# Expert stage with fixed first blocks, a ring of weight pairs filled from the out-projection on, and token numbers found by one-hot products

## Chip, core and metric

The kernel runs on one core of one Trainium2 chip. The metric is the device time of the whole kernel in microseconds, from the first to the last instruction and what lies around them; lower is better. All arrays are fp32 unless said otherwise.

## What is computed

One step of a one-layer decoder trunk with model width 1024, for 512 prompt tokens and 32 sample tokens (8 sequences of 4) with a paged cache of 2048 past positions each. Cut to what matters here:

```
h = RMSNorm(x)
q, k, v, gates = split(h @ w_in)
o_a = sparse attention over the top keys picked by an indexer   (prompt and sample)
o_b = block-sparse attention over the top blocks                (prompt and sample)
x  += (sigmoid(gate_a) * (o_a @ w_br_a) + sigmoid(gate_b) * (o_b @ w_br_b)) @ w_out
h2  = RMSNorm(x) * g_ffn
per token: best of 4 groups, then the top 2 of its 8 experts, with weights w1, w2
x  += sum over both experts of  w * ((silu(h2 @ w_gate[e]) * (h2 @ w_up[e])) @ w_down[e])
y   = RMSNorm(x) * g_final
```

There are 32 experts of hidden width 256: w_gate and w_up are 1024 x 256 each, w_down 256 x 1024, so 3.1 MB per expert and 100.7 MB for all. 544 tokens with 2 experts each give 1088 assignments.

## The kernel before

The work runs in stages, each a block in which every engine has its own list of instructions. Between two blocks all engines meet; in several places semaphores are reset there as well. Nothing is reordered by a planner: the order on each engine and each queue (SP's, ACT's and POOL's) is the order written, and waits are on semaphores written by hand. `Chain` (L130) makes each VectorE instruction wait for the one before it.

`project` (L269) normalises x and multiplies by w_in for the attention columns. At its start POOL also writes 25 blocks of rows with the number NOROW into `slot_table` in HBM (L387 to L391), beside the first loads of x, constants and weights. `prompt` does the prompt's attention.

`sample` (L906) does the sample's attention. TensorE goes through NS steps: `turn(n)` transposes gathered keys, `scores(n-1)` multiplies them by queries; ScalarE copies each turned tile out. VectorE picks the top keys by repeated rounds of eight (`rounds`), merges the lists (`largest_of_all`), counts, and lets TensorE add up the counts in `places_left`, which stands in front of step COUNT_AT (L925). VectorE's list is `rounds(0, 24)`, `mask(0)`, `normalise(0)` (which waits for ScalarE's `exps(0)`, L1255), the other eight rounds, `largest_of_all`, `bias_of_choice`, `mask(1)` and so on (L1398 to L1410). The bias is used by `spread` (L1101). The value gathers are issued by POOL as slots of the ring of eight come free. At the end `weigh(3, 1)` is the last product with gathered values, and then TensorE turns the outputs o_b and o_a into obT and oaT (L1191 to L1201).

`merge` (L1419) makes u column block by column block (8 blocks of 128 columns). Per block j TensorE makes the two gate products (i = 0, 1) and the two branch products (i = 2, 3), each in two halves of 272 tokens. For the gate products hT and the gate weights are split by VectorE into a high and a low part in fp32r, and each product is three (L1545); the branch products are plain fp32 (L1536). SP loads gate weights into one buffer and branch weights into two. ScalarE makes the sigmoids, VectorE multiplies and adds. Then, in the same block, comes the out-projection, token tile by token tile (5 tiles): uT times w_out, added to x (which has been loaded over hT), RMSNorm, store of h2 and of x to HBM by SP (L1511, L1513), transposes of h2 and the router product.

`route` (L1694) is a chain of small VectorE instructions: group and expert choice as one-hot arrays E[0], E[1]; a product with a triangular matrix counts the earlier assignments (L1750); from it the place of each assignment in a table of blocks of 64 rows, one or more blocks per expert. POOL scatters the token numbers into `slot_table` by ten indirect DMAs (L1853). `block_expert` names the expert of each block, `npair` the number of block pairs.

`experts` (L1858) reads the slot table back (L1903) and loops over the pairs at run time (Fori). SP loads, per turn, the gate and up weights of the two blocks' experts in two parts of 4 k-tiles and the down weights; there is one buffer of each, so a part is loaded again once the products that read it are done. POOL gathers the pair's 128 rows of h2 and scatters the result rows. TensorE turns the rows (L1965), makes gate and up (L1975: 32 products in which the two blocks use the two halves of the array's columns), turns the hidden rows (L1981) and makes down (L1991). Gather, products and scatter of a turn follow one another, except that the next gather is issued once the rows are turned.

`combine` (L2027) loads the expert rows, adds them with w12 to x (loaded again from HBM by SP at the end of `experts`, L1921), normalises and stores.

## Time and profile before

| | us |
|---|---|
| median of 3 runs (range) | 1274.71 (1272.75 to 1276.52) |
| the profiled execution | 1271.91 |
| its span, first to last instruction | 1270.1 |
| TensorE busy, of the span | 1000.6 (79%) |
| VectorE / ScalarE / GpSimd busy | 423.9 / 291.5 / 183.7 |
| granted TensorE clock, mean | 0.883 |
| moved by DMA | 253.05 MB, mean 199 GB/s |

The stages on this clock: project and prompt until 336, sample until 622, merge from 624 to 795, out-projection until 880, routing and the first loads until 935, expert loop until 1240, combine until the end.

How to read the rows. A timeline row has the start, the length (of a merged run, from its first start to its last end), the engine, the line of the kernel, the operation, what it writes and reads, the shape, the count, and in brackets how long the engine had been idle before it and what ended that. PE is TensorE's products, PEld its weight loads, DVE VectorE, ACT ScalarE, POOL GpSimd, SPq the DMA issues of SyncE. A row of a stretch has start and end, the length, the busy time of PE, PEld, DVE, ACT and POOL with their counts, the granted TensorE clock (1.00 is 2.4 GHz, 0.50 is 1.2 GHz), the mean busy share of the 16 DMA engines, and the GB/s that they moved.

### The profile page before, as it was taken

How to read it: one execution, taken by the hardware profiler on the slowest of the kernel's cores; microseconds unless marked ns; L12 is line 12 of the kernel's file. 1: busy time of each engine (PE TensorE's matmuls, PEld its weight loads, DVE VectorE, ACT ScalarE, POOL GpSimd, SP SyncE). 2: the span in 40 equal slices, each digit the busy share in tenths (PEclk: the TensorE clock that was granted, in tenths of full speed). 3: DMA queues.
4: the chain of work that ended last, by engine and by line, in shares of the span. 5: the costliest groups of instructions: out<-in, count | busy, mean ns of one | idle time of the engine just before them, and what ended most of it. 6: DMA issues, size and time to landing. Idle time of an engine off the chain costs nothing. (4 is left out here: it accounts for less than half of the span.)

```text
span 1270.1 us, 14844 instructions
## 1 busy us (share of the span) xinstructions
PE 1000.6 (79%) x5669; PEld 582.1 (46%) x5669; DVE 423.9 (33%) x909; ACT 291.5 (23%) x451; POOL 183.7 (14%) x246
## 2 busy tenths in 40 slices
PE   5999998888899978876499999996057777777750
PEld 4544443667656645123399999453022222222220
DVE  2214886444349282220333330122401111111116
ACT  3122212444247747010100000111001110110112
POOL 4100100120013324333100000000301111111110
PEclk9999999998599979687799999997569988898895
DMA  8212201223149948998583330110199999999985
GB/s 292 84 67 75 94 1 38 59 65 109 67 144 336 374 150 303 399 387 308 151 286 86 98 89 1 45 72 26 19 316 373 372 349 369 350 366 366 366 311 211
DMA packets 147382, 253.05 MB, mean 199 GB/s; under 512 B 20096, under 2 KB 111632, under 8 KB 139008
## 3 DMA queue, kind: packets, MB, share of 16 engines
q1 hardware_dynamic: 124800, 149.05, 35.2%
q0 software_dynamic: 21904, 101.02, 21.9%
q10 hardware_dynamic: 624, 2.23, 0.5%
q8 instruction: 38, 0.62, 0.2%
q14 instruction: 16, 0.13, 0.0%
HBM read 240.46 MB, written 20.19 MB: 205 GB/s over the span
## 5 line engine op out<-in xcount | busy, mean ns | idle before, releaser
L679 PE MATMUL bank<-ring,hT 128*128 128x512 f32 (+1 forms) x384 | 162.5, 578 | 1.6 <-DMA ring<-in_w_in 1.6
L1975 PE MATMUL bank<-w_gate_up,xT 128*64 128x512 f32 x512 | 127.7, 651 | 32.6 <-DVE xT L2016 20.9
L679 PEld LDWEIGHTS bank<-ring,hT 128*128 128x128 f32 x384 | 72.7, 194 | 81.9 <-issue 71.4
L1245 ACT COPY kT_s<-bank 128x1024 f32<-128x1024 f32 (+1 forms) x90 | 85.7, 997 | 64.0 <-PE bank L1030 63.9
L1030 PEld LDWEIGHTS bank<-consts,ring 128*128 128x128 f32 x704 | 79.8, 146 | 41.3 <-ACT kT_s L1245 35.1
L1030 PE MATMUL bank<-consts,ring 128*128 128x128 f32 x704 | 91.7, 284 | 2.7 <-PEq L219 1.7
L1975 PEld LDWEIGHTS bank<-w_gate_up,xT 128*64 128x64 f32 x512 | 38.1, 149 | 112.2 <-issue 91.4
L1545 PE MATMUL bank<-hT_hi,gate_w_hi 128*128 128x272 f32 x256 | 76.1, 297 | 14.8 <-DVE gate_w_lo L1645 14.8
L1991 PE MATMUL bank<-w_down,hidT 128*64 128x512 f32 x256 | 70.1, 697 | 9.8 <-DVE hidT L2023 8.5
L1545 PE MATMUL bank<-hT_hi,gate_w_lo 128*128 128x272 f32 x256 | 74.6, 291 | 0.0
L1545 PE MATMUL bank<-hT_lo,gate_w_hi 128*128 128x272 f32 x256 | 74.6, 291 | 0.0
L1583 PE MATMUL bank<-w_o,uT 128*128 128x512 f32 (+1 forms) x160 | 69.5, 593 | 1.7 <-DVE uT L1664 1.7
L1149 PE MATMUL bank<-ring,wT_s 128*32 128x512 f32 x256 | 48.4, 926 | 21.3 <-DMA ring<-in_cache_v_b,rows_b 21.3
L2016 DVE COPY xT<-bank 128x1024 f32<-128x1024 f32 x16 | 19.6, 1224 | 123.9 <-PE bank L1965 123.9
L1965 PE MATMUL bank<-consts,xg 128*128 128x128 f32 x128 | 19.8, 305 | 49.8 <-DMA xg<-h_rows,id 49.7
L1545 PEld LDWEIGHTS bank<-hT_hi,gate_w_hi 128*128 128x128 f32 x256 | 49.1, 192 | 15.2 <-DVE gate_w_lo L1645 14.9
L2019 DVE TENSOR_TENSOR sgm<-sgm,bank 128x256 f32<-128x256 f32 x16 | 6.7, 421 | 147.5 <-ACT sgm L2004 147.5
L1853 POOL DMA_INDIRECT slot_table<-rt_ids,slot x10 | 10.9, 1089 | 296.3 <-DVE rt_ids L1834 293.6
L1545 PEld LDWEIGHTS bank<-hT_lo,gate_w_hi 128*128 128x128 f32 x256 | 49.1, 192 | 0.3
L1545 PEld LDWEIGHTS bank<-hT_hi,gate_w_lo 128*128 128x128 f32 x256 | 49.0, 191 | 0.0
L265 POOL DMA_INDIRECT ring<-in_cache_k_b,rows_b x32 | 30.0, 937 | 128.4 <-PE bank L1030 98.7
L1583 PEld LDWEIGHTS bank<-w_o,uT 128*128 128x128 f32 (+1 forms) x160 | 27.5, 174 | 40.9 <-issue 40.9
(329 smaller groups left out, 1378.0 us busy)
## 6 DMA issues: line engine op xcount, KB each, us to landing
w_gate_up<-in_w_e_gate SPq DMA_DIRECT2D x64, 512.0 KB, 7.9
w_gate_up<-in_w_e_up SPq DMA_DIRECT2D x64, 512.0 KB, 8.9
w_down<-in_w_e_down SPq DMA_DIRECT2D x32, 1024.0 KB, 10.4
ring<-in_w_in SPq DMA_DIRECT2D x5, 2048.0 KB, 8.3
gate_w<-in_w_in SPq DMA_DIRECT2D x16, 512.0 KB, 5.2
w_o<-in_w_out SPq DMA_DIRECT2D x1, 4096.0 KB, 14.9
ring<-in_x_prompt SPq DMA_DIRECT2D x4, 512.0 KB, 8.4
branch_w<-in_w_br_a SPq DMA_DIRECT2D x16, 128.0 KB, 3.4
```

The lines of the kernel that those rows point to most:

```text
L265: pool.indirect_dma_start(s.ring[:, r, 0:wide], None, cache.rearrange("g (p e) h d -> (g p) (e h d)", e=e), bass.IndirectOffsetOnAxis(inde ...
L679: last = nc.tensor.matmul(bank[:, n % 4, 0:WID[g]], s.hT[:, k, t * P:(t + 1) * P], w[:, gi % 2, k, 0:WID[g]], start=(k == 0), stop=(k == K ...
L1030: last = nc.tensor.transpose(bank[:, u, e * P:(e + 1) * P], ring[:, slot, at:at + P], ident)
L1149: last = nc.tensor.matmul(out[rows_at(u), :], probT[m][:, c * nslot + e, rows_at(u)], ring[:, slot, e * w:(e + 1) * w], start=(c == 0 and ...
L1245: nc.scalar.copy(kT[:, n % 2, u, :], bank[:, u, :]).then_inc(kT_kept, 1)
L1545: last = nc.tensor.matmul(out, l, m, start=(k == 0 and c == 0), stop=(k == KD - 1 and c == 2))
L1583: last = nc.tensor.matmul(bank[0:rows, n % 4, :], uT[:, k, t * P:t * P + rows], wo[:, k, half * 512:half * 512 + 512], start=(k == 0), sto ...
L1853: pool.indirect_dma_start(s.slots, bass.IndirectOffsetOnAxis(ap=s.slot[0:rows, k, t:t + 1], axis=0), ids[0:rows, k, t, :], None).then_inc( ...
L1965: last = nc.tensor.transpose(bank[:, k // 4, k % 4 * PAIR:(k % 4 + 1) * PAIR], xg[:, k * P:(k + 1) * P], const(s, "ident"))
L1975: last = nc.tensor.matmul(bank[r, 2, :], xT[:, kk, r], wgu[:, u, part, k, :], start=(kk == 0), stop=(kk == KD - 1))
L1991: last = nc.tensor.matmul(bank[r, 4 + half, :], hidT[:, f, r], wd[:, u, f, half * 512:half * 512 + 512], start=(f == 0), stop=(f == KF - 1))
L2016: nc.vector.tensor_copy(xT[:, :, :].rearrange("p (b k) r -> p b (k r)", b=2), bank[:, 0:2, :])\
```

## The change

In words, with the new names:

- `project`: the 25 zero-row stores, `slot_table` and `residual_rows` are gone. The constants lose 80 columns and gain 193.
- `sample`: SP gets a block that loads the branch weights of column block 0 into `s.bw`. COUNT_AT is NI + 38 instead of NI + 33; `exps(0)` comes one step earlier; VectorE's order changes; `weigh(3, 1)` moves behind the turning of o_b.
- `merge` ends before the out-projection. Column block 0 does the branches first and its gate products plain, from an unsplit buffer `gw0` that lies in w_out's place; gate loads run one block further ahead; w_out is loaded at block 3, x at block 5.
- `project_out`, a new block, is the out-projection as it was, except that x is not stored, POOL stores h2, and SP issues gate/up weights of pairs 0 and 1 and down weights of pair 0.
- `experts` now holds the routing too. Blocks 0 to 31 are the first 64 rows of expert 0 to 31, whatever their count; further rows go to overflow blocks (at most 16). The first 15 pairs are unrolled, with weights in a ring of three gate/up pairs (two in `s.early`, one in w_out's place) and two down pairs (one in uT's place). The sixteenth pair and the overflow pairs are a run-time loop with at least one turn. The routing places give a row and a block number for each assignment; ten pairs of products of one-hot matrices put token number + 1 (+ 2048 for the second choice) into PSUM, and six VectorE instructions make gather and scatter numbers of it. Rows and results have two buffers each; the next pair's rows are turned between gate/up and the hidden rows.
- `combine` reads x from where it stayed in SBUF.

Sampling:

```diff
@@ sample @@
-    COUNT_AT = NI + 33
+    COUNT_AT = NI + 38
...
+        @block.sync
+        def _(sp):
+            for half in range(2):
+                sp.dma_start(s.bw[half * HD:half * HD + HD, 0, 0, :, :],
+                             a["w_br_a"][0, half * PAIRS * HD:(half + 1) * PAIRS * HD, 0:P]
+                             .rearrange("(j d) n -> d j n", d=HD)).then_inc(first_in, 16)
+            sp.dma_start(s.bw[:, 0, 1, :, :], a["w_br_b"][0, :, 0:P].rearrange("(j p) n -> p j n", p=P))\
+                .then_inc(first_in, 16)
+            sp.wait_ge(first_in, 48)
...
-            weigh(3, 1)
             pe.wait_ge(spread_read, 10)
             for x in "ba":
+                if x == "a":
+                    weigh(3, 1)
...
-                if n == NI + 26:
+                if n == NI + 25:
                     exps(0)
...
             mask(0)
+            rounds(FIRST_ROUNDS, TOPK_S // 8 - FIRST_ROUNDS)
             normalise(0)
-            rounds(FIRST_ROUNDS, TOPK_S // 8 - FIRST_ROUNDS)
             largest_of_all()
+            mask(1)
             bias_of_choice()
-            mask(1)
             normalise(1)
```

Merge and out-projection:

```diff
@@ merge @@
+        gw0 = wo[:, 0:2, :].rearrange("p g (k n) -> p g k n", k=KD)
+        ORDER = [(2, 3, 0, 1)] + [(0, 1, 2, 3)] * (NCH - 1)
...
             gates(0)
-            branches(0)
+            gates(1)
             branches(1)
-            gates(1)
-            sp.dma_start(wo[:, :, :], a["w_out"][0].rearrange("(k p) n -> p k n", p=P)).then_inc(out_in, 16)
-            sp.wait_ge(hT_split, KD)
-            sp.dma_start(xp, a["x_prompt"][0].rearrange("(t p) d -> p t d", p=P)).then_inc(x_in, 16)
-            sp.dma_start(xs[:, :], a["x_sample"].rearrange("b q d -> (b q) d")).then_inc(x_in, 16)
             for c in range(2, NCH):
                 gates(c)
                 sp.wait_ge(prod_done, 4 * (c - 1))
                 branches(c)
+                if c == 3:
+                    sp.wait_ge(hT_split, KD)
+                    sp.dma_start(wo[:, :, :], a["w_out"][0].rearrange("(k p) n -> p k n", p=P)).then_inc(s.out_in, 16)
+                if c == 5:
+                    sp.dma_start(s.xp, a["x_prompt"][0].rearrange("(t p) d -> p t d", p=P)).then_inc(s.res_in, 16)
+                    sp.dma_start(s.xs[:, :], a["x_sample"].rearrange("b q d -> (b q) d")).then_inc(s.res_in, 16)
...
+                            if j == 0:
+                                last = nc.tensor.matmul(out, gw0[:, i, k, :], s.hT[:, k, rows],
+                                                        start=(k == 0), stop=(k == KD - 1))
+                                continue
@@ project_out, SP and POOL @@
+            sp.dma_start(gf[:, :], a["g_ffn"].to_broadcast([P, D])).then_inc(gf_in, 16)
+            sp.dma_start(wr[:, :, 0:NG], a["w_grp"][0].rearrange("(k p) n -> p k n", p=P)).then_inc(r_in, 16)
+            sp.dma_start(wr[:, :, NG:NG + NE], a["w_exp"][0].rearrange("(k p) n -> p k n", p=P)).then_inc(r_in, 16)
+            load_gate_up(sp, s, a, 0)
+            load_gate_up(sp, s, a, 1)
+            load_down(sp, s, a, 0)
...
+            for t in range(TT):
+                rows = rows_of(t)
+                pool.wait_ge(h2_ready, t + 1)
+                pool.dma_start(s.h2[t * P:t * P + rows, :], h2[0:rows, t % 2, :]).then_inc(h2_stored[t % 2], 16)
```

Experts, loads and token numbers (`load_gate_up` issues four loads of 1 MB, `load_down` two):

```diff
@@ experts, SP @@
+            load_gate_up(sp, s, a, 2)
+            load_down(sp, s, a, 1)
+            for p in range(NGU, LAST):
+                sp.wait_ge(gu_done, p - NGU + 1)
+                load_gate_up(sp, s, a, p)
+                sp.wait_ge(y_done, p - 1 - NWD + 1)
+                load_down(sp, s, a, p - 1)
+            sp.wait_ge(y_done, LAST - 1 - NWD + 1)
+            load_down(sp, s, a, LAST - 1)
+            sp.wait_ge(turns_ready, 1)
+            turns = sp.value_load(nturn[0:1, 0:1], min_val=1, max_val=1 + MAXOB // 2)
+            with sp.Fori(0, turns) as i:
...
+                load_gate_up(sp, s, a, LAST, e)
+                sp.wait_ge(y_done, LAST - NWD + 1)
+                sp.wait_ge(down_free, i + 1)
+                load_down(sp, s, a, LAST, e)
@@ experts, PE @@
+            for k in range(2):
+                pe.wait_ge(places_ready, k + 1)
+                for t in range(TT):
+                    for u in range(2):
+                        column = blocks_are[k][:, t, :].rearrange("p (b u) -> p u b", u=2)[:, u, :]
+                        last = nc.tensor.matmul(bank[half(u), 7, 0:MAXP], rows_are[k][:, t, :], column,
+                                                start=(k == 0 and t == 0), stop=(k == 1 and t == TT - 1))
+            last.then_inc(found, 1)
...
+            turn_tokens(0, 16)
+            for p in range(LAST):
+                gate_up(p, p, 64 * (p // NGU + 1), gu_done)
+                turn_tokens(p + 1, 16 * ((p + 1) // 2 + 1))
+                turn_hidden(p)
+                down(p, p, 32 * (p // NWD + 1), p - 1 if p >= 2 else None, y_done)
@@ experts, DVE, behind the choice of experts @@
+            for k in range(2):
+                link(nc.vector.tensor_tensor(rows_are[k], rowf[:, k, :].unsqueeze(2).to_broadcast([P, TT, BLK]),
+                                             const(s, "iota").unsqueeze(1).to_broadcast([P, TT, BLK]), ALU.is_equal))
+                link(nc.vector.tensor_tensor(blocks_are[k], blkf[:, k, :].unsqueeze(2).to_broadcast([P, TT, NBLK]),
+                                             const(s, "iota")[:, 0:NBLK].unsqueeze(1).to_broadcast([P, TT, NBLK]),
+                                             ALU.is_equal))
+                link(nc.vector.tensor_tensor(blocks_are[k], blocks_are[k],
+                                             const(s, f"word{k}").unsqueeze(2).to_broadcast([P, TT, NBLK]), ALU.mult),
+                     places_ready)
```

VectorE's chain between the sum of the counts and these lines: base (6 instructions), the places (9 of 160 elements a partition, and small sums), the overflow blocks of each expert (2 of 256, a scan and small ones), block number by comparison with 47 block starts (2 of 470) and the row in the block.

## Rows read from the trace of the kernel before

**Rows 1.** Stretches: length, busy PE PEld DVE ACT POOL, granted clock, DMA share, GB/s.

```profile
795.00:880.00 85.00, 82.44 (x280) 40.89 (x280) 15.04 (x26) 13.01 (x31) 0.00 (x0) 0.98 0.14 53
...
880.00:935.00 55.00, 3.53 (x14) 2.76 (x16) 21.13 (x71) 2.99 (x4) 13.61 (x16) 0.50 0.30 88
...
935.00:1240.00 305.00, 221.56 (x920) 78.13 (x920) 38.61 (x63) 41.57 (x47) 38.53 (x63) 0.90 1.03 355
```

**Rows 2.** Short stretches of the expert loop, same columns.

```profile
936.00:938.00 2.00, 2.00 (x6) 0.48 (x4) 0.00 (x0) 0.00 (x0) 0.00 (x0) 0.50 1.04 409
...
948.00:950.00 2.00, 2.00 (x8) 0.87 (x6) 0.00 (x0) 0.00 (x0) 0.00 (x0) 0.50 1.10 349
...
953.85:1027.37 73.52, 53.12 (x232) 19.17 (x232) 9.96 (x16) 12.07 (x14) 10.78 (x17) 0.95 1.07 370
```

**Rows 3.** Timeline, POOL and PE, first 25 us.

```profile
1.49 13.44 POOL L391 DMA_DIRECT2D slot_table<-zrow  x25 [0.32 <-POOL zrow L387]
...
17.21 7.40 PE L679 MATMUL bank<-ring,hT 128*128 128x328 f32 x16 [1.56 <-DMA ring<-in_w_in]
```

**Rows 4.** Timeline, DVE, sampling.

```profile
445.70 0.17 DVE L1384 RECIPROCAL inv_s<-total_s 128x1 f32<-128x1 f32 x1 [12.25 <-ACT lg_b L1208]
```

**Rows 5.** Timeline, PE, sampling, in order of time.

```profile
372.95 1.05 PE L1053 MATMUL bank<-kT_s,q_b 128*32 128x512 f32 x4
...
469.94 0.59 PE L1097 MATMUL bank<-counts,consts 128*128 128x1 f32 x2 [9.25 <-DVE counts L1335]
...
470.82 1.95 PE L1030 MATMUL bank<-consts,ring 128*128 128x128 f32 x8
...
477.12 1.97 PE L1030 MATMUL bank<-consts,ring 128*128 128x128 f32 x16
```

**Rows 6.** Timeline, PE, end of sampling.

```profile
613.34 3.54 PE L1149 MATMUL bank<-ring,kT_s 128*32 128x128 f32 x64 [3.93 <-DMA ring<-in_cache_v_a,rows]
```

**Rows 7.** Timeline, PE, ACT and PEld, merge.

```profile
636.37 0.59 PE L1545 MATMUL bank<-hT_hi,gate_w_hi 128*128 128x272 f32 x1 [14.79 <-DVE gate_w_lo L1645]
...
650.59 0.62 ACT L1602 ACTIVATE sig<-bank 128x544 f32<-128x544 f32 x1 [5.41 <-PE bank L1545]
...
669.99 0.62 ACT L1602 ACTIVATE sig<-bank 128x544 f32<-128x544 f32 x1 [5.41 <-PE bank L1545]
...
766.63 3.52 PEld L1536 LDWEIGHTS bank<-oaT,branch_w 128*128 128x128 f32 x16
```

**Rows 8.** Timeline, first instructions behind two block boundaries.

```profile
624.40 0.21 DVE L1641 MEMSET logit<- 128x180 f32 x1 [2.10 <-PEq L207]
...
880.19 1.28 ACT L1742 ACT_TABLE_LOAD   x1 [0.84 <-PEq L224]
```

**Rows 9.** Timeline, DVE and PE, routing and first turn.

```profile
892.14 0.09 DVE L1804 MEMSET rt_base<- 128x32 f32 x1 [0.81 <-PE bank L1751]
...
900.74 0.82 DVE L1831 TENSOR_SCALAR rt_ids<-consts 128x640 int32<-128x640 f32 x1
...
901.60 0.17 DVE L1834 CAST rt_ids<-consts 128x5 int32<-128x5 f32 x1
...
931.51 1.94 PE L1965 MATMUL bank<-consts,xg 128*128 128x128 f32 x8 [39.52 <-DMA xg<-h_rows,id]
...
934.84 10.09 PE L1975 MATMUL bank<-w_gate_up,xT 128*64 128x512 f32 x32 [1.40 <-DVE xT L2016]
```

**Rows 10.** DMA issues (count, median us from issue to landing).

```profile
xg<-h_rows,id POOLq DMA_INDIRECT x17, 7.1
ring<-in_cache_k_idx,rows POOLq DMA_INDIRECT x16, 3.3
```

**Rows 11.** Timeline, PE, a down product group in the loop.

```profile
1040.46 3.65 PE L1991 MATMUL bank<-w_down,hidT 128*64 128x512 f32 x16 [0.61 <-DVE hidT L2023]
```

**Rows 12.** Waits of PE, 880 to 1240 us (total, times, longest).

```profile
PE bank L1981 <- DVE hid L2021: 23.7, 16, 1.5
```

**Rows 13.** Timeline, ACT, last copy of y.

```profile
1231.69 1.01 ACT L2007 COPY y<-bank 128x1024 f32<-128x1024 f32 x1 [5.84 <-PE bank L1991]
```

More of the change, by code:

```diff
@@ L1520, in _ @@
             for j in range(NCH):
[L1521 removed]
+                for i in ORDER[j]:
                     if i < 2:
[L1523 to L1525 removed]
+                        if j == 0:
+                            pe.wait_ge(gate0_in, 32)
+                        else:
+                            pe.wait_ge(gate_split, 2 * (j - 1) + i + 1)
+                    elif i == 2 and j >= 1:
+                        pe.wait_ge(br_in[j % 2], 48 * ((j + 1) // 2))
                     if j >= 1:
@@ L1547, in _ @@
                     last.then_inc(prod_done, 1)
-            pe.wait_ge(out_in, 16)
-            pe.wait_ge(u_ready, NCH)
+        @block.scalar
+        def _(act):
+            for j in range(NCH):
+                if j >= 2:
+                    act.wait_ge(u_ready, j - 1)
+                for i in range(2):
+                    act.wait_ge(prod_done, 4 * j + ORDER[j].index(i) + 1)
+                    nc.scalar.activation(sg[:, j % 2, i, :].rearrange("p (b r) -> p b r", b=2),
+                                         bank[:, 2 * i:2 * i + 2, 0:HALF], ACT.Sigmoid).then_inc(sig_ready, 1)
@@ new lines, in _, with split, split_gates @@
+        @block.vector
+        def _(dve):
+            link = Chain(dve, chain_v)
+            link(nc.vector.memset(s.logit[:, :, :], 0.0))
+            def split(hi, lo, v, ready):
+                link(nc.vector.tensor_copy(hi.bitcast(F32R), v))
+                link(nc.vector.tensor_tensor(lo.bitcast(F32R), v, hi, ALU.subtract), ready)
+            def split_gates(j):
+                dve.wait_ge(gate_in, 32 * j)
+                for g in range(2):
+                    split(gh[:, j % 2, g, :, :], gl[:, j % 2, g, :, :], gw[:, g, :, :], gate_split)
+            for k in range(KD):
+                split(hTh[:, k, :], hTl[:, k, :], s.hT[:, k, :], hT_split)
+            for j in range(NCH):
+                if j + 1 < NCH:
+                    split_gates(j + 1)
+                for i in (0, 1):
+                    dve.wait_ge(prod_done, 4 * j + ORDER[j].index(i + 2) + 1)
+                    dve.wait_ge(sig_ready, 2 * j + i + 1)
+                    dst = (uT[:, j, :] if i == 0 else part[:, :]).rearrange("p (b r) -> p b r", b=2)
+                    link(nc.vector.tensor_tensor(dst, sg[:, j % 2, i, :].rearrange("p (b r) -> p b r", b=2),
+                                                 bank[:, 4 + 2 * i:6 + 2 * i, 0:HALF], ALU.mult), mul_done)
+                link(nc.vector.tensor_tensor(uT[:, j, :], uT[:, j, :], part[:, :], ALU.add), u_ready)
@@ L1744, in _, with sigmoid, keep @@
             nc.scalar.activation(ratio[:, :], ratio[:, :], ACT.Exp).then_inc(gexp_ready, 1)
-        @block.tensor
-        def _(pe):
-            pe.wait_ge(both_ready, 1)
-            flat = both[:, :, :].rearrange("p t e -> p (t e)")
-            nc.tensor.matmul(bank[:, 0, 0:TT * NE], const(s, "before"), flat, start=True, stop=True)
-            nc.tensor.matmul(bank[:, 1, 0:TT * NE], s.ones[:, :], flat, start=True, stop=True).then_inc(sum_done, 1)
+            def sigmoid():
+                nc.scalar.activation(sgm[:, :], bank[:, 2, 0:DE], ACT.Sigmoid).then_inc(sig_ready, 1)
+            def keep(slot, done, count):
+                act.wait_ge(done, count)
+                nc.scalar.copy(y[:, slot % 2, :].rearrange("p (b n) -> p b n", b=2),
+                               bank[:, 4 + 2 * (slot % 2):6 + 2 * (slot % 2), :]).then_inc(y_ready, 1)
+            for p in range(LAST):
+                act.wait_ge(gu_done, p + 1)
+                sigmoid()
+                if p >= 2:
+                    act.wait_ge(y_stored[p % 2], 16 * (p // 2))
+                keep(p, y_done, p + 1)
+            act.wait_ge(turns_ready, 1)
+            turns = act.value_load(nturn[0:1, 0:1], min_val=1, max_val=1 + MAXOB // 2)
+            with act.Fori(0, turns) as i:
+                act.wait_ge(gu_free, i + 2)
+                sigmoid()
+                act.wait_ge(y_stored[LAST % 2], i * 16 + 16 * (LAST // 2))
+                keep(LAST, down_free, i + 2)
         @block.vector
@@ L2027, in combine @@
+            with dve.Fori(0, turns) as i:
+                hidden(i + LAST)
+                keep_tokens(i + (LAST + 1), LAST)
 def combine(nc, s, a, o):
```

622 lines of the change are left out of this document (299 added, 323 removed).

## Prediction

> **What bounds the kernel now.** I read the page first (the span in 40 slices), then stretches, then the timeline of each stretch. From 935 to 1240 us, in the 16 turns of the expert loop, the DMA share is 1.03 and TensorE is busy 222 of 305 us [rows 1]: the weights' stream sets the pace. When it does not pause it moves 370 GB/s; alone, gate and up weights (1 KB pieces) run at about 350 and down weights (4 KB pieces) at about 410 [rows 2]. Ahead of it, 880 to 935, no engine works much and DMA has a share of 0.30; and 795 to 880, the out-projection, TensorE is busy 82 of 85 us at a DMA share of 0.14 [rows 1]. So the stream is idle for 140 us and then binds for 300. That is the place to look; the other parts of the change touch waits of TensorE.
>
> The reference, run on its inputs, gives 1088 assignments over 32 experts, the largest expert has 50, none is empty. So 32 blocks, 16 pairs, both before and after, and the new loop makes one turn. All 100.7 MB of weights still come once.
>
> **The change, part by part** (times on the clock of the profiled execution).
>
> *Start.* 25 stores of zero rows leave POOL's queue (1.6 MB in 13.4 us) while TensorE's first projection product waits for w_in until 17.2 [rows 3]. At the stream's 370 GB/s [rows 2] they are worth 4.4 us of loads; bounds 0 (something else comes last) and 5. I take 3.0, nearer the upper end because the product's wait ends with a DMA. The constants grow by 113 columns (58 KB, 0.2 us of stream, under the same loads).
>
> *Sampling, the count.* VectorE's normalise(0) waited 12.25 us for ScalarE [rows 4]; the rounds behind it, and so the counts, were late, and TensorE stood 9.25 us at places_left [rows 5]. After it the clock was at the lower level: from 470.82 to 477.12 it did 12 transposes and two steps' scores in 6.3 us, which at 0.12 us a transpose and 1.0 us a step's scores, as elsewhere [rows 5], is 3.4; and places_left itself costs 0.9 instead of 0.4. The new order runs all rounds first (counts ready near 458) and asks five steps later, near 473; exps(0) comes one step earlier on ScalarE, between the same copies. Gain 9.25+2.85+0.4 = 12.5. mask(1) now stands before bias_of_choice: it needs the last b scores (about 467) and takes 10 us, so the bias comes near 482, before its first use near 491: nothing late. The gathers of values start as soon as slots are freed, so they shift too. Bounds 0 (a later wait takes it) and 13.
>
> *Sampling, the tail.* weigh(3,1) waited 3.9 us for gathered values [rows 6]; the 16 b products (0.12 each, 2.0 us) now lie in it. But the a products then wait for VectorE's last read: gain 1.2 (0 to 2.0).
>
> *Merge.* TensorE waited 14.8 us for splits of hT and gates, then took 14 us for the gates and 7.3 for branches; ScalarE's second sigmoid of column block 0 is at 650.6, block 1's at 670.0, so block 1 begins at 657.6 [rows 7]. Now branch weights are there, branches go first (from 624.5, 32 products; 16 weight loads take 3.52 us at the higher clock [rows 7], so 0.227 a product, double for the first 4.2 us): until 633.9. The first gates are unsplit: 32 products at 0.227, 7.3 us, not 96 split ones, which take the rest of a block, 19.4-7.3 = 12.1, until 641.2. Gate loads (1 MB, first in SP's queue: 3 us of stream and a start) are there by about 630; splits for block 1 end at 638.3, both before need. Gain 16.4 (12 to 17). w_out and x move later in SP's queue, behind the branches of blocks 3 and 5; there are 19 us a block and w_out's 4.2 MB need 11 at 370: hidden. Without that cover it would cost its 11. Block 0's branch weights (0.5 MB) come during sampling from SP's queue, which was empty there.
>
> *A new block boundary* between merge and out-projection. Boundaries idle 0.84 and 2.10 us [rows 8]. Route and expert blocks fuse, but their boundary is counted below. Cost 1.8 (0.8 to 4, with the clock falling).
>
> *Out-projection.* SP issues 10.5 MB (two gate/up pairs, one down) in a stretch with DMA share 0.14: 28 us of stream inside 85, nothing waits. Stores of h2 go to POOL's queue, whose engine is empty; the residual's stores are gone. 6.3 MB more go out at 880 (17 us) and are in at about 902. Cost 0; if the covers fail, 45 us (16.8 MB at 370).
>
> *Routing.* Before, VectorE's chain from 892.14 ended at 901.8, then ten scatters, a boundary, a table read, a gather: first transposes at 931.51, first gate/up product at 934.84 [rows 9]. Now: by size (5 elements a partition cost 0.2, 640 cost 0.86 with the gap [rows 9], 160 by the line between them 0.36) the new chain is 12 ops of up to 32 (2.3), 9 of 160 (3.2), two of 256 (0.9), two of 470 (1.4), and per k 320, 240, 240 elements (2.8): 10.6 us, from 891.9 to 902.6. Ten products (1.5), six small ops (1.3): 905.4. Gather without a stream beside it: 3.3 us, as the index gathers; beside the stream it was 7.1 [rows 10], the upper bound. Then 3.3 us to the first product, as before: 912.1. Gain 22.7 (18 to 26). w12 and the block table move behind: covered by the gather and later turns. Without that cover, 4 us.
>
> *Experts.* The stream restarts when gate_up(0) ends, 10.5 us later (10.1 [rows 9], at the lower clock). Left are 13 gate/up pairs and 14 down pairs, 83.9 MB, and 8.1 MB of gathers and scatters: 92.0 MB at 370 = 249 us. Is it fed? Load p waits for product p-3, and a full-clock pair takes TensorE 3.65 for the 16 down products, 7.1 for gate and up (32 products of the same size, 7.3 by twice that) and 1.2 for transposes [rows 5, 11], plus 1.6 of waits (1.5 for hid before, part now under the transposes [rows 12]), 13.6 us, below 18.5 per pair: each load is issued before the stream reaches it. VectorE's copy of xT stands behind hidT's, under the down product. SP's wait for y_done has only the next down load behind it, with one gate/up pair in flight. ScalarE's copy of y waits for the store two pairs back. After the last byte: gate_up(15), hidden, down, copy: 12 us with a dip of the clock. Sum 10.5+249+12 = 271.5 against 934.84 to 1232.70 = 297.9 [rows 9, 13]. Gain 26.4 (16 to 45).
>
> First the row: a stream that does not pause is 370 GB/s. By the Trainium skill, DMA: Bandwidth & Descriptors, Specifications, a core's share of HBM is about 358 GB/s; the stream would then be 257 us, 8 more. The rows disagree [rows 2], the 410 most.
>
> *Combine.* Residual stays on chip: five loads less, which had been under the last turn. Gain 0; one more reset: cost 1.0.
>
> **Sum**: -3.0-12.5-1.2-16.4+1.8-22.7-26.4+1.0 = -79.4. The profiled execution took 1271.9 us (span 1270.1), 2.8 below the median of the runs: 1192.5 on its own scale, 1195 on the median's. I give 1193.
>
> **Rivals.**
> 1. *The stream keeps its old mean*, 355 GB/s over the whole stage [rows 1], pauses included: 92.0/0.355 = 259, +10: 1203. For it: 1 KB pieces again. Against: pauses came from single buffers. Chance 0.12. The Trainium skill's 358 GB/s (DMA: Bandwidth & Descriptors, Specifications) comes to nearly this.
> 2. *The sampling wait only moves*: bias_of_choice is now 7 us later, values become the wait. +12.5: 1205. Against: the slack worked out above. 0.10.
> 3. *The stream is faster*, 400 GB/s with larger loads: 230 us, -19: 1174. 0.08.
> 4. *The clock decides (slower)*. TensorE waits for weights about 5 us per pair. At the lower clock the pair costs 2 x 11.95 + 1.6 = 25.5 us. If the clock were low throughout, the last copy would be at 912+16 x 25.5+2 = 1322 instead of 1184: 1330. Slower than now needs 80 us more, 5.0 per pair over 16.9: 21.9, that is 70% of the work at the lower level. For it: the first product took 10.1 us instead of 7.1 [rows 9, 11]. Against: in the same regime of waits the mean clock is 0.90 [rows 1]. Half of the work low gives 19.5 a pair, 42 more in all: 1235. Chances 0.05 for this half case (0.01 of it near no change), 0.04 for slower. The Trainium skill, TensorE: Matmul & The Clock Gate, HAM oscillation, tells of a kernel that started every tile cold after a DMA wait; the trace agrees only in part, by that 0.90.
> 5. *It does not do what it says*: the early loads are not early (queue or bias loads held up): +45: 1238. 0.04.
>
> **Numbers.** The forecast has 0.57 with its own range 1178 to 1207; the likeliest is the predicted time. Low end 1172 holds rival 3; high end 1220 holds 1 and 2 and part of the half case. About 0.3% (4 us) is what a measurement tells from no change. Faster: all but rival 4's slower case and the 0.01: 0.95; same 0.01; slower 0.04.
>
> **What would show it.** no 9 us wait at the counts; the first merge product near 624.5-16.7 = 608, and from it to the second column block 17 us, where 33 lay between the block's start and that point; first gate/up product 32 us after the out-projection's end, not 55; DMA share above 1 from ten us after it for about 250 us; time from first gate/up to the last y copy 271. If the last is near 298 the experts' term is wrong; if the granted clock in the stage is below 0.8, rival 4 is at work; a wait of TensorE for down weights in each pair is expected, one for gate/up weights is not.

## The result and the profile after

The changed kernel took 1191.5 us (median of four, 1189.3 to 1194.8), the kernel before 1275.6: ratio 0.9346, 95% interval 0.9318 to 0.9374. On two other chips the changed kernel had 1195.8 against 1273.7 (0.9393, 0.9342 to 0.9445) and 1199.7 against 1273.9 (0.9420, 0.9374 to 0.9466). Forecast were 1193 and a range of 1172 to 1220. One of e11's six runs below, at 1189.3 us, was slow as a whole, with a granted clock of 0.887 where the others had 0.900 to 0.916, and is left out of e11's median.

The profiled execution took 1191.2 us, with a span of 1189.3; before, 1270.1. Cut at the first or last product of each stage, the difference of 80.8 us lies here (all times are TensorE's, in us; each row runs from the point that the row above names to its own):

| from ... to | before | after | difference | forecast |
|---|---|---|---|---|
| start, first projection product | 17.2 | 13.0 | -4.2 | -3.0 |
| first query product of sampling | 327.2 | 322.9 | -4.3 | 0 |
| end of the last score product | 158.3 | 147.2 | -11.1 | -12.5 |
| end of sampling's last product | 118.8 | 112.5 | -6.4 | -1.2 |
| first out-projection product | 173.8 | 165.3 | -8.5 | -14.6 |
| first gate/up product | 139.5 | 118.9 | -20.6 | -22.7 |
| end of the last down product | 296.7 | 271.1 | -25.6 | -26.4 |
| end | 38.5 | 38.5 | 0.0 | +1.0 |

The sum is right to 1.4 us, and that is partly luck: the merge gave 6 us less than forecast, and the two stages for which little or nothing was forecast (to the first query product, and the second part of sampling) gave 9.5 us more.

Stretches of the changed kernel, with the columns of [rows 1]: the out-projection, the routing, the stretch from about the landing of the last early weights to the end of the first gate/up products, and the expert stage.

```profile
760.83:845.43 84.60, 82.30 (x280) 40.71 (x280) 14.83 (x25) 13.01 (x31) 2.71 (x5) 0.98 0.47 159
845.43:879.69 34.26, 5.93 (x52) 4.89 (x52) 21.27 (x77) 2.99 (x4) 2.82 (x4) 0.50 0.62 202
862.00:888.00 26.00, 12.81 (x80) 6.41 (x80) 11.50 (x36) 0.00 (x0) 3.09 (x3) 0.60 0.27 91
888.00:1140.00 252.00, 195.88 (x852) 71.32 (x852) 35.98 (x60) 20.94 (x30) 28.58 (x30) 0.89 1.05 364
```

The out-projection takes as long as before, 83.6 us from its first product to the end of its last router product (83.8 before), with 159 GB/s beside it instead of 53: the early loads cost nothing there. From 888 on the stream does not pause (share 1.05) and moves 364 GB/s for 252 us. But from 867, when the last early weights land, to 888.3, when SP issues the next ones, it stands, because every buffer is full and none is free before the first gate/up products have ended.

TensorE's timeline at the counts, and then at the merge's first column block:

```profile
465.25 0.38 PE L1114 MATMUL bank<-counts,consts 128*128 128x1 f32 x2
465.49 0.36 PE L1115 MATMUL bank<-counts,consts 128*128 128x1 f32 x2
...
597.88 6.31 PE L1523 MATMUL bank<-oaT,branch_w 128*128 128x272 f32 x16 [2.33 <-PEq L217]
604.03 3.83 PE L1523 MATMUL bank<-obT,branch_w 128*128 128x272 f32 x16
607.69 14.83 PE L1528 MATMUL bank<-hT,w_o 128*128 128x272 f32 x64
622.16 0.49 PE L1534 MATMUL bank<-hT_hi,gate_w_hi 128*128 128x272 f32 x1
```

The wait of 9.25 us of [rows 5] is gone, and the products of the counts take 0.4 us and not 0.6: the clock did not fall. In the merge, look at the count of L1528 (a count is of records, the instructions as the profile lists them). The 32 plain gate products of the code (2 gates, 2 halves, 8 k-tiles) are 64 records and take 14.8 us, not the 7.3 that the prediction gave them. Column block 1 begins 24.3 us after the first product, not 17.

The routing, first on VectorE and then on TensorE:

```profile
849.42 0.35 DVE L2025 TENSOR_TENSOR logit<-logit,router_bias 128x180 f32<-128x180 f32 x1 [9.43 <-DMA router_bias<-in_b_exp]
...
857.86 0.09 DVE L2052 MEMSET rt_base<- 128x32 f32 x1 [1.44 <-PE bank L1917]
...
868.03 0.41 DVE L2087 TENSOR_TENSOR branch_w<-branch_w,consts 128x240 f32<-128x240 f32 x1
...
870.96 0.18 DVE L2098 SCALAR_TENSOR_TENSOR ids<-id_second,id_found 128x24 int32<-128x24 f32 x1
```

```profile
876.34 1.97 PE L1930 MATMUL bank<-consts,oaT 128*128 128x128 f32 x8 [6.58 <-DMA oaT<-h_rows,ids]
879.69 8.53 PE L1939 MATMUL bank<-early,obT 128*64 128x512 f32 x32 [1.39 <-DVE obT L2124]
```

From the start of the base at 857.86 to the last one-hot matrix is 10.6 us and to the token numbers 13.3, to 0.2 us as worked out from sizes. The gather then takes 5.2 us until its rows can be turned, not 3.3. The first line shows a wait that both kernels have: the chain starts 4.0 us behind the start of the block (3.3 before), because the router's bias is loaded there.

In the expert stage, a pair with its wait (TensorE), the last copy of y (ScalarE, the answer to [rows 13]), and the list of TensorE's waits from 860 to 1160 us:

```profile
949.54 6.01 PE L1958 MATMUL bank<-early,hidT 128*64 128x512 f32 x16 [7.34 <-DMA early<-in_w_e_down]
955.38 7.03 PE L1939 MATMUL bank<-w_o,obT 128*64 128x512 f32 x32
```

```profile
1150.92 1.01 ACT L1989 COPY branch_w<-bank 128x1024 f32<-128x1024 f32 x1 [5.79 <-PE bank L1958]
```

```profile
PE bank L1958 <- DMA early<-in_w_e_down: 23.8, 5, 7.3
PE bank L1958 <- DMA uT<-in_w_e_down: 23.3, 6, 5.0
...
PE bank L1939 <- DMA early<-in_w_e_up: 1.0, 1, 1.0
```

As forecast, TensorE waits for down weights and, but for 1.0 us at the last pair, not for gate and up. The forecast had this wait in each pair; it is in 11 of 16. In nine pairs the down products behind it run at the lower level in part (5.2 to 6.7 us instead of 3.65; 6.0 above), and it costs nothing: the gate/up products start at once behind them, and the next pair's down weights are waited for again, 2.8 to 5.0 us, in all nine.

### The profile page after: what moved, and what is told of

It reads as the page before. It is cut to its first block and busy times, and to the rows that moved or that the text cites. A ratio compares the mean times of both kernels' runs of the same rounds, so it can differ in the third digit from the quotient of the medians.

```text
span 1189.3 us, 14006 instructions
## 1 busy us (share of the span) xinstructions
PE 981.8 (83%) x5685; PEld 577.0 (49%) x5685; DVE 420.8 (35%) x912; ACT 272.6 (23%) x436; POOL 155.2 (13%) x183
## 3 DMA queue, kind: packets, MB, share of 16 engines
q0 software_dynamic: 21408, 101.05, 23.1%
## 5 line engine op out<-in xcount | busy, mean ns | idle before, releaser
L686 PEld LDWEIGHTS bank<-ring,hT 128*128 128x128 f32 x384 | 72.0, 192 | 79.4 <-issue 70.4
L1939 PE MATMUL bank<-early,obT 128*64 128x512 f32 x352 | 79.0, 602 | 2.4 <-DVE obT L2124 1.4
L1534 PE MATMUL bank<-hT_hi,gate_w_hi 128*128 128x272 f32 x224 | 65.9, 294 | 0.0
L1534 PE MATMUL bank<-hT_hi,gate_w_lo 128*128 128x272 f32 x224 | 64.6, 288 | 0.0
L1534 PE MATMUL bank<-hT_lo,gate_w_hi 128*128 128x272 f32 x224 | 64.5, 288 | 0.0
L1958 PE MATMUL bank<-early,hidT 128*64 128x512 f32 x128 | 39.4, 772 | 25.6 <-DMA early<-in_w_e_down 23.8
L1958 PE MATMUL bank<-uT,hidT 128*64 128x512 f32 x128 | 39.4, 773 | 24.5 <-DMA uT<-in_w_e_down 23.3
L1939 PEld LDWEIGHTS bank<-early,obT 128*64 128x64 f32 x352 | 26.1, 140 | 53.7 <-issue 50.0
L1989 ACT COPY branch_w<-bank 128x1024 f32<-128x1024 f32 x16 | 16.2, 1012 | 153.0 <-PE bank L1958 153.0
L1880 POOL DMA_INDIRECT expert_rows<-branch_w,ids x15 | 15.1, 1006 | 227.2 <-ACT branch_w L1989 227.2
L853 ACT ACTIVATE prob<-bank,ntop 128x512 f32<-128x512 f32 (+3 forms) x64 | 30.2, 523 | 53.5 <-DVE ntop L893 53.5
## 6 DMA issues: line engine op xcount, KB each, us to landing
early<-in_w_e_down SPq DMA_DIRECT2D x16, 1024.0 KB, 12.7
```

Of the source, the lines that this page charges most:

```text
L686: last = nc.tensor.matmul(bank[:, n % 4, 0:WID[g]], s.hT[:, k, t * P:(t + 1) * P], w[:, gi % 2, k, 0:WID[g]], start=(k == 0), stop=(k == K ...
L853: nc.scalar.activation(prob[:, m % 3, half, 0:width(t)], bank[:, 2 * (m % 2) + half, 0:width(t)], ACT.Exp, bias=ntop[:, m % 4, half:half + ...
L1534: last = nc.tensor.matmul(out, l, m, start=(k == 0 and c == 0), stop=(k == KD - 1 and c == 2))
L1880: pool.indirect_dma_start(s.y, bass.IndirectOffsetOnAxis(ap=column, axis=0), y[:, p % 2, :], None, bounds_check=2 * NTOK - 1, oob_is_err=F ...
L1939: last = nc.tensor.matmul(bank[half(u), 2, :], xT[:, slot % 2, k, half(u)], gate_up_at(s, slot)[:, u, k, :], start=(k == 0), stop=(k == KD ...
L1958: last = nc.tensor.matmul(bank[half(u), 4 + 2 * (slot % 2) + n, :], hidT[:, f, half(u)], down_at(s, slot)[:, u, f, n * 512:n * 512 + 512], ...
```

## Experiments

Each edit is made to the changed kernel.

**e1 and e10, the zero rows.** A scratch array takes them:

```diff
+            nc.gpsimd.memset(zrow[:, :], NOROW).then_inc(zero_ready, 1)
+            pool.wait_ge(zero_ready, 1)
+            for k in range(25):
+                pool.dma_start(s.slots[k * P:(k + 1) * P, :], zrow[:, :]).then_inc(zero_done, 16)
```

> The changed kernel with the 25 stores of zero rows (1.6 MB) back on POOL's queue at the start; nothing else differs. In the changed kernel the first projection product begins at 13.0 us, before at 17.2, and sampling's first transposes come 7.8 us earlier. Theory 1 (the stores took the loads' place in the DMA engines, and TensorE starts later and at the lower clock): first projection product at 17, whole kernel +5 to +8 us. Theory 2 (my prediction's size): +3 us. Theory 3 (the earlier start is something else, the stores are free): within 1 us.

Measured: 1203.6 us, ratio 0.9475 (0.9441 to 0.9509), 12.3 above e3 below, which ran on the same chip and whose time is the changed kernel's. But the profiled execution had 1194.5 at a granted clock of 0.910, and the four others 1203.4 to 1206.5 at 0.895 to 0.900. So it was taken again with the changed kernel (e9) beside it.

> The changed kernel itself again, beside the next three: 1188 to 1198 us, first gate/up product to last down product 271 to 273 us, out-projection to first gate/up product 118.4 to 118.9 us, as in its two traces.

> The zero-row stores back at the start, as in e1, where the trace showed 5.3 us at the second token tile of the projection (24.06 against 18.74) and the medians of two different chips 8 to 12. Theory 1 (the trace has it all, the rest was the chip and the clock in the prompt's stage): +5 to +6 us against the changed kernel on the same chip. Theory 2 (the later start also costs clock in the stages that follow): +8 us or more.

Measured: e10 1205.5 us (0.9465, 0.9421 to 0.9509), e9 1199.7 (0.9420, 0.9374 to 0.9466; 1.7 above what was expected, with its two stages, 272.2 and 118.5 us, as expected): 5.8 apart, as theory 1 has it, and the intervals overlap. TensorE's timelines, e9 first, then e10:

```profile
14.36 5.09 PE L686 MATMUL bank<-ring,hT 128*128 128x328 f32 x16
19.29 1.04 PE L652 MATMUL bank<-consts,ring 128*128 128x128 f32 x8
```

```profile
15.63 6.31 PE L694 MATMUL bank<-ring,hT 128*128 128x328 f32 x16 [1.24 <-DMA ring<-in_w_in]
21.78 1.04 PE L660 MATMUL bank<-consts,ring 128*128 128x128 f32 x8
```

With the stores the wait for w_in is back and the first 16 products run partly at the lower clock; the second tile begins 2.5 us later (in e1, against the changed kernel's first trace, 5.3). The first product begins at 15.6 and, in e1, at 17.5 us, in the eleven traces of the changed kernel and its versions without the stores at 13.0 to 14.6, with no wait for w_in. So it is shown that the stores hold up the first loads: theory 3 is out. The size is not settled. The timelines have 2.5 to 5.3 us, the medians 5.8 and 12.3, and the difference goes with the granted clock of later stages, which theory 2 claims and which varies by itself as well (last section).

**e2, sampling's order.**

```diff
-    COUNT_AT = NI + 38
+    COUNT_AT = NI + 33
-                if n == NI + 25:
+                if n == NI + 26:
             mask(0)
-            rounds(FIRST_ROUNDS, TOPK_S // 8 - FIRST_ROUNDS)
             normalise(0)
+            rounds(FIRST_ROUNDS, TOPK_S // 8 - FIRST_ROUNDS)
             largest_of_all()
-            mask(1)
             bias_of_choice()
+            mask(1)
```

> The changed kernel with sampling's old order: the counts asked five steps earlier, exps(0) one step later, normalise(0) between the rounds, bias_of_choice ahead of mask(1). Theory 1 (the wait at the counts comes back and nothing behind it hides it): a wait of 8 to 10 us of TensorE at the product of the counts and +11 to +13 us in all, of which 12.5 was my term. Theory 2 (a later wait for gathered values takes most of it, as the values' stage got only 3 us shorter): +3 to +8 us.

```profile
473.71 0.59 PE L1114 MATMUL bank<-counts,consts 128*128 128x1 f32 x2 [9.26 <-DVE counts L1353]
```

Measured: 1208.5 us (0.9500, 0.9466 to 0.9534), against 1191.3 for e3 on the same chip. The wait came back, 9.26 us where it had been 9.25: theory 1, though more than its 11 to 13 us in all. From the first query product to the end of the last score product the stage takes 158.2 us, as before the change (158.3); the changed code takes 147.2 to 150.2 in its twelve other traces (every other run here leaves that stage as it is). From there to the end of sampling it is 115.3, inside the 109 to 119 of the others. So the order is worth 8 to 11 us and nothing behind it takes them back. The values' stage differs from trace to trace by as much as the 5 us that it seemed to gain. The medians are 17 apart; the rest is not explained by the edit's own stage, and stages before it differ as much by themselves (last section).

**e3, the first gates.** Split in three as in the other blocks:

```diff
-                        if j == 0:
-                            pe.wait_ge(gate0_in, 32)
-                        else:
-                            pe.wait_ge(gate_split, 2 * (j - 1) + i + 1)
+                        pe.wait_ge(gate_split, 2 * j + i + 1)
...
-                            if j == 0:
-                                last = nc.tensor.matmul(out, gw0[:, i, k, :], s.hT[:, k, rows],
-                                                        start=(k == 0), stop=(k == KD - 1))
-                                continue
```

> The changed kernel, branches of column block 0 still first, but its gate products split in three as in every other block, with its gate weights loaded into the common buffer. A plain product is two records of 0.227 us in the trace, 32 of them 14.5 us; a split one is three of 0.126, 32 of them 12.1 us, but they can start only when VectorE has split hT and the weights, about 12 us after the block begins, 2 us behind the branches. Theory 1 (the plain form gains nothing, all of the gain comes from the branches' place): column block 1 begins within 1 us of the changed kernel's 24.3 us after the first branch product, time within 1 us. Theory 2 (my prediction's: plain gates save the splits' wait and 4.8 us): +5 us or more.

```profile
603.61 3.83 PE L1518 MATMUL bank<-obT,branch_w 128*128 128x272 f32 x16
609.53 0.39 PE L1527 MATMUL bank<-hT_hi,gate_w_hi 128*128 128x272 f32 x1 [2.08 <-DVE gate_w_lo L1548]
```

Measured: 1191.3 us (0.9367, 0.9334 to 0.9400). The wait for the splits is 2.1 us, and the split products win it back: ScalarE's second sigmoid of the block comes 24.60 us after the first branch product, in the changed kernel 24.68. Plain gates gain nothing; all of the merge's 9 us are the branches that stand where the wait was. Theory 1.

**e4, late loads.**

```diff
@@ project_out, SP @@
-            load_gate_up(sp, s, a, 0)
-            load_gate_up(sp, s, a, 1)
-            load_down(sp, s, a, 0)
@@ experts, SP, behind the loads of the biases @@
+            load_gate_up(sp, s, a, 0)
+            load_gate_up(sp, s, a, 1)
+            load_down(sp, s, a, 0)
```

> The changed kernel with the 10.5 MB of early weights (two gate/up pairs, one down pair) loaded at the start of the routing and not in the out-projection. Theory 1 (the stream is a fixed amount of work behind routing: every MB loaded early is time saved): +28 us. Theory 2 (the stream stands idle from 862 to 888 us in the changed kernel, because all buffers are full until the first gate/up products are done; the 10.5 MB would mostly fall into that gap): 16.8 MB from 846 on at 365 GB/s end at 892, 4 us after the time at which the stream restarts now: +3 to +8 us. Theory 3 (the first gate/up product or the gather of rows is delayed by the stream beside it): up to 4 us more than theory 2.

The gather now runs beside the stream:

```profile
875.65 1.97 PE L1930 MATMUL bank<-consts,oaT 128*128 128x128 f32 x8 [9.86 <-DMA oaT<-h_rows,ids]
```

And the stretch from 862 to 888, in which the changed kernel moved 91 GB/s, is full:

```profile
862.00:888.00 26.00, 13.50 (x85) 6.97 (x86) 7.86 (x28) 0.39 (x1) 3.09 (x3) 0.62 1.08 364
```

Measured: 1197.9 us (0.9432, 0.9394 to 0.9470), 6.6 above e3 on the same chip. In the trace, out-projection to first gate/up is 122.1 us (+3.2: TensorE waits 9.86 us and not 6.58 for the rows, and the first two gathers take 7.5 and 7.7 us to land where they took 4.2 and 4.4), and the expert stage is 276.7 (+5.6). Theories 2 and 3, not 1: moving 10.5 MB out of an idle stretch costs 7 to 9 us and not 28, since the stream has another idle stretch, 867 to 888, that takes most of them. The out-projection without the early loads beside it takes 83.8 us, with them 83.6.

**e5 and e6, the ring.** e5 is the changed kernel again.

> The changed kernel itself, on the chip of the next three kernels, to compare them with: 1188 to 1195 us. In the profiles so far the stage from the prompt's attention to sampling's first score product is up to 11 us longer or shorter with the same instructions, at another granted clock; a span of this run within that.

Measured: 1195.8 us, 0.8 above what was expected, and 272.8 us for the expert stage. e6 has

```diff
-NGU, NWD = 3, 2
+NGU, NWD = 2, 2
...
-            load_gate_up(sp, s, a, 2)
             load_down(sp, s, a, 1)
```

> The changed kernel with two gate/up buffers and not three (both still loaded in the out-projection; w_out's place stays empty; one more wait ahead of the last pair's loads). Theory 1 (stream bound; a ring of two keeps it fed, as a pair's products take 13 us of the stream's 17; only the 4.2 MB loaded during routing come later): 4.2 MB at 365 GB/s = +11 to +12 us, DMA share above 1.0 as before. Theory 2 (the third buffer is what keeps the stream from pausing): pauses of 2 us or more in each of 14 pairs on top, +35 us or more, DMA share below 1.0.

```profile
890.00:960.00 70.00, 54.45 (x248) 20.75 (x246) 9.59 (x16) 5.59 (x8) 8.11 (x8) 0.90 0.99 335
960.00:1150.00 190.00, 140.71 (x578) 48.51 (x576) 23.98 (x40) 13.97 (x20) 19.25 (x19) 0.86 1.05 364
```

Measured: 1209.5 us (0.9507, 0.9443 to 0.9571), +13.7; the stage 285.5, +12.7. The second row has the same 364 GB/s as with three buffers; only its start is thinner. Theory 1, with a little more than its 11 to 12 us: the third buffer is worth the 4.2 MB that it holds early (11.5 us at 365 GB/s), not a steadier stream.

**e7 and e11, the pieces.** Each partition takes neighbouring rows of the weights instead of every 128th, and the tokens are turned with the same stride, so the sums are over the same terms in another order:

```diff
-    return w.rearrange("p (u k n) -> p u k n", u=2, k=KD)
+    return w.rearrange("p (u c k n) -> p u c k n", u=2, c=2, k=KD)
...
-            w = a[name][0].rearrange("e (k p) n -> p e k n", p=P)
+            w = a[name][0].rearrange("e (p k) n -> p e k n", p=P)
...
-                                               xg[:, slot % 2, k * P:(k + 1) * P], const(s, "ident"))
+                                               xg[:, slot % 2, :].rearrange("p (q k) -> p k q", k=KD)[:, k, :],
+                                               const(s, "ident"))
```

and likewise for down (not in e11).

> The changed kernel with the experts' weights laid out so that a partition's share of a load is one piece of 8 KB in HBM and in SBUF (partition p holds rows 8p to 8p+7 of gate or up, 2p and 2p+1 of down, instead of every 128th row; the tokens and hidden rows are turned with the same stride). Before, gate/up pieces are of 1 KB and down pieces of 4 KB, and moved at about 350 and 410 GB/s. Theory 1 (the stream binds and its rate goes by the size of the pieces): gate/up rise to about 400: 54.5 MB behind the restart in 136 instead of 152 us, the stage 15 to 20 us shorter, DMA rate 390 to 410. Theory 2 (the mix is limited elsewhere, at 365 to 370 whatever the pieces): within 3 us. Theory 3 (strided reads of the rows slow the transposes): they take longer than 1.1 us for eight, hidden under the stream's waits.

> As e7, but only gate and up get pieces of 8 KB; down keeps its pieces of 4 KB. Theory 1 (the 1 KB pieces of gate and up were the slow ones, 4 KB is long enough): same as e7 within 2 us: first gate/up product to last down product 245 to 247 us, rate about 410 GB/s. Theory 2 (the rate still rises from 4 to 8 KB): e7 keeps 4 us or more of its 27.

The stage's stretch of e7, of e11, and of e12 below:

```profile
888.00:1110.00 222.00, 185.46 (x833) 72.86 (x833) 35.82 (x60) 19.54 (x28) 27.28 (x27) 0.93 1.00 413
```

```profile
888.00:1110.00 222.00, 185.10 (x814) 69.53 (x812) 33.57 (x56) 18.92 (x28) 26.34 (x26) 0.92 0.98 398
```

```profile
890.00:1110.00 220.00, 182.19 (x816) 72.03 (x818) 34.44 (x58) 19.58 (x28) 27.34 (x27) 0.92 1.01 416
```

Measured: e7 1172.5 us (0.9227, 0.9170 to 0.9283), 23.4 under e5 on the same chip, stage 245.2 (-27.6), more than the 15 to 20 us of its theory 1. e11 1175.8 us (0.9242, 0.9187 to 0.9298), 24.0 under e9, stage 249.0 (-23.1). The stream is what binds, and its rate goes with piece length: 364 GB/s with gate and up in pieces of 1 KB, 398 with 8 KB, 413 with down in 8 KB as well. The last step is worth 2 to 4 us in the stage (249.0 against 246.8 in e12 and 245.2 in e7); e11's stage came out between what the two theories wanted, and the times of the two, from different chips, don't part them. The share column falls from 1.05 to 1.00 while more is moved: share is occupation of the DMA engines, not bytes. A row's rate over its share is then what a fully occupied set of engines moves, an estimate: 349/1.10 = 317 GB/s with pieces of 1 KB and 409/1.04 = 393 with 4 KB [rows 2], 413/1.00 = 413 with 8 KB. So the engines are occupied in every version, and long pieces carry more in that time. The edit also changes the order in which a load goes through HBM; no run here parts that from the length. Eight strided transposes take 1.16 us, straight ones 1.09. By the Trainium skill, DMA: Bandwidth & Descriptors, Specifications, transfers of 512 B and more reach line rate; here they do not at 1 KB.

**e8, the bias.** Loaded at the start of the out-projection:

```diff
@@ experts, SP @@
-            sp.dma_start(bias[:, 0:NG], a["b_grp"].to_broadcast([P, NG])).then_inc(bias_in, 16)
-            sp.dma_start(bias[:, NG:], a["b_exp"].to_broadcast([P, NE])).then_inc(bias_in, 16)
@@ project_out, SP @@
+            sp.dma_start(s.bias[:, 0:NG], a["b_grp"].to_broadcast([P, NG])).then_inc(bias_in, 16)
+            sp.dma_start(s.bias[:, NG:], a["b_exp"].to_broadcast([P, NE])).then_inc(bias_in, 16)
```

> The changed kernel with the router's biases loaded at the start of the out-projection and not at the start of the routing, where VectorE waits for them until 4.0 us after the block begins. Theory 1 (that wait is the head of the routing's chain): first gate/up product 3.0 to 3.6 us earlier after the out-projection, stream restarts as much earlier, total -3 us. Theory 2 (something else is as late): within 1 us.

```profile
855.39 0.35 DVE L2025 TENSOR_TENSOR logit<-logit,router_bias 128x180 f32<-128x180 f32 x1 [5.36 <-PEq L248]
```

Measured: 1199.0 us (0.9427, 0.9371 to 0.9482), 3 above e5. But the wait for the DMA is gone, and from the out-projection to the first gate/up product it is 114.8 us, where the ten traces without this edit and with the loads early have 118.0 to 119.1; the expert stage is 272.7 as ever. Its profiled execution had lost 5 us to e5 already at the out-projection's first product (770.9 against 765.8), ahead of the edit. The step is shown, -3.6 us; the total can't show it.

**e12, both.** e7 and e8 together.

> e7 and e8 together: long pieces for all experts' weights, router biases loaded in the out-projection. e7 took 26 to 28 us off the experts' stage (245.2 us where the changed kernel has 271.1 and 272.8), e8 3.7 us off the way from the out-projection to the first gate/up product (114.8 against 118.4 to 118.9). Theory 1 (they add up, since one lies ahead of the stream's restart and one behind it): 29 to 31 us under the changed kernel on the same chip. Theory 2 (at the higher rate TensorE begins to bind and part is lost): under 26 us.

Measured: 1166.1 us (0.9163, 0.9116 to 0.9209), 33.6 under e9 on the same chip, their intervals apart. Out-projection to first gate/up 114.7, stage 246.8: -3.8 and -25.4 to e9. They add up in the stages, 29.2 us, as theory 1 has it; the other 4 us of the medians lie in no stage that was edited. This version is faster than both kernels, by 8.4% than the one before.

## Why the prediction was right, and where not

**Right by its own steps.** Early loads: free beside the out-projection. Routing: the chain of VectorE to 0.2 us, from two rows and a line between them. The gather was sized at 3.3 us from issue to landing, as the index gathers, and took 5.2 from the numbers to the turning, 1.9 of the 2.1 that this term lacks: it took 4.2 us to land, and POOL issued it 0.9 us behind the numbers, a step for which the sum had nothing. Experts: 271.5 forecast, 272.2 measured to the end of the copy, and here errors cancel. The restart came after 8.6 us and not 10.5. From it to the last landing, at 1142.7, are 254.4 us and not 249. Behind that come 9.3 us and not 12. The rate was 364 GB/s: the unpaused stretch (370) and the stage's mean (rival 1, 355 GB/s and 259 us) miss it by about as much, one on each side, so the run does not bear out the choice between them. The figure of the Trainium skill (DMA: Bandwidth & Descriptors, Specifications), 358 GB/s, stands 6 below the measured rate and 55 below that of e7, so it is no limit here, with one core running. Rival 3, a faster stream from larger loads, did not come: the loads were of 1 MB instead of 512 KB, in the same pieces of 1 KB, at 364 GB/s. Rival 4, the clock, did not decide: 0.89 in the stage, and the slow down products all lie ahead of weights that are late.

**Wrong: the merge.** The step that failed is "The first gates are unsplit: 32 products at 0.227, 7.3 us, not 96 split ones". The 0.227 is the price of one record, from 16 records of weight loads, and it was taken for that of one product of the code. A branch has 4 k-tiles and 2 halves, 8 products, so a plain fp32 product is two records, 0.454 us; three split ones at 0.126 are 0.378. The plain form is the slower one, 14.5 against 12.1 us. With that, the prediction's own chain gives 624.5 + 9.4 + 14.5 = 648.4 for block 1, a gain of 9.2; measured are 8.5 with the new boundary in it, which added 0.8 (2.56 us of wait ahead of the first out-projection product, 1.72 before). The branches' own price was right, because there records were divided by records.

**Mis-sized: sampling.** 12.5 forecast, 8 to 11 shown by e2. The wait of 9.25 us is the same in e2 and is gone without it; how much came of the 2.85 for the clock behind it can't be told from the spread of 3 us between traces. Rival 2 (a later wait takes its place) did not come.

**Mis-sized: sampling's tail.** 1.2 forecast. From the end of the second last group of value products to the end of sampling it is 12.2 us before and 8.6 after: the wait for gathered values is 1.96 us instead of 3.93, and the 64 products of weigh(3, 1) behind it take 1.96 and not 3.54, a term of the clock that the sum did not have. All thirteen traces with the change have 6.6 to 11.6 us here, so the gain is 0.5 to 5.6 us; no run moved weigh(3, 1) alone.

**Mis-sized: the late-load rival.** Rival 5 had 45 us for early loads that fail, bytes over rate. e4 moved 10.5 of the 16.8 MB and paid 7 to 9 us instead of 28. The prediction had the stream's restart at the end of the first gate/up products, and did not draw the conclusion that there is a gap ahead of it which absorbs what comes late. So the early loads are worth less than their bytes, and the third buffer about its bytes (e6: 12.7 us in the stage for 11.5 of stream), because without a buffer to take them nothing can be loaded in that gap.

**Luck.** 4.3 us of the difference lie from the first projection product to sampling's first query product, where only the 1.5 us of a faster clock behind the start belong to the change. The difference of the medians is 84.1 us here and 77.9 and 74.1 on the two other chips, and the forecast of 79.4 lies among them.

## What to carry to other kernels

Before a product is priced, divide a group's records by the products that the code writes: here a plain fp32 product was two, and its split into three the cheaper form. Bytes loaded early save their time only if the stream has no later gap that would have taken them. Where a stream binds, look at the length of its pieces as well as at buffers and order: here it gave 25 to 28 us of the expert stage, as much as the ring and its early loads did (25.6).

## What was not expected

The same instructions of the prompt's attention take different times in different executions. Windows from 240 to 330 us of the changed kernel, of e4 and of e2, none of which differs there:

```profile
240.00:330.00 90.00, 75.94 (x480) 60.65 (x476) 38.41 (x64) 39.13 (x84) 12.25 (x13) 0.81 0.24 77
```

```profile
240.00:330.00 90.00, 73.93 (x500) 59.88 (x496) 41.68 (x78) 40.68 (x86) 12.74 (x14) 0.87 0.26 81
```

```profile
240.00:330.00 90.00, 83.75 (x449) 67.35 (x450) 36.38 (x59) 36.01 (x75) 12.25 (x13) 0.68 0.24 77
```

The granted clock is 0.81, 0.87 and 0.68, and from the first projection product to the first query product it is 322.9, 318.5 and 333.9 us. It is a stretch where TensorE waits often and shortly: idle for 14 of the 90 us in the first row, never for more than 1.4 at a time. The spread of 15 us is wider than six of the eight forecasts of the table, so a term is read from its own stage, cut at its own first and last product, and medians of two kernels are compared on the same chip only. By the Trainium skill, TensorE: Matmul & The Clock Gate, HAM oscillation, a kernel with pauses can fall to the lower level again and again; these windows agree, and show that how much of the time it spends there is not the same from one execution to the next. Why is open; no run here was made for it.
